# Key norms of the delta rule from ScalarE's row sums over token-major transposes, in place of half of TensorE's products with ones

## What is computed

```python
def l2_normalize(x):
    return x * lax.rsqrt(jnp.sum(x * x, axis=-1, keepdims=True) + NORM_EPS)
...
qkv_a = jax.nn.silu(causal_depthwise_conv(qkv_a, gdn_conv_w))
q_a, k_a, v_a = [a.reshape(b_, s_, GDN_HEADS, GDN_HEAD_DIM).astype(f32) for a in jnp.split(qkv_a, 3, axis=-1)]
q_a = l2_normalize(q_a) * (GDN_HEAD_DIM ** -0.5)
k_a = l2_normalize(k_a)
...
kb = k * beta[..., None]
a_low = jnp.where(strict, jnp.einsum('bhnid,bhnjd->bhnij', kb, k) * decay, 0.0)
ia = a_low + jnp.eye(c, dtype=q.dtype)
u = lax.linalg.triangular_solve(ia, v * beta[..., None], left_side=True, lower=True, unit_diagonal=True)
```

## Time and profile before

| What | Value |
|---|---|
| median of 3 runs | 890.04 us |
| the profiled execution | 890.07 us, its span 888.3 us |
| PE busy | 874.8 us (98%), 5624 instructions |
| DVE busy | 586.1 us (66%) |
| ACT busy | 440.2 us (50%) |
| POOL busy | 51.3 us (6%) |
| chain that ended last | PE 87%, DVE 8%, ACT 2%, issue 1%, DMA 1% |
| granted clock of PE, mean | 0.998 |

### The profile page before, as it was taken

How to read it: one execution, slowest core, us unless ns; L and a number is a source line. 1 busy time by engine, 2 the same in 40 slices (tenths; PEclk the granted TensorE clock), 3 DMA queues, 4 the chain that set the end, 5 groups by cost and what they waited for, 6 DMA issues and landing times.

```text
span 888.3 us, 13795 instructions
## 1 busy us (share of the span) xinstructions
PE 874.8 (98%) x5624; PEld 759.6 (86%) x5624; DVE 586.1 (66%) x898; ACT 440.2 (50%) x644; POOL 51.3 (6%) x78
## 2 busy tenths in 40 slices
PE   8999999999999999999999999999999999999997
PEld 6888999898999888888889999877788888888885
DVE  5785664565656755555686997956477667777544
ACT  6644444753345544544485652466254555555442
POOL 1000000000020110000020015200000100000000
PEclk9999999999999999999999999999999999999999
DMA  9757644456454554556757683412555556665441
GB/s 294 239 190 227 223 144 142 143 166 183 127 184 153 184 179 153 175 183 198 263 145 248 159 174 95 144 49 49 143 190 181 180 184 190 189 190 190 166 166 48
DMA packets 127813, 151.67 MB, mean 171 GB/s; under 512 B 16983, under 2 KB 93142, under 8 KB 127750
## 3 DMA queue, kind: packets, MB, share of 16 engines
q1 hardware_dynamic: 127466, 150.44, 53.8%
q10 hardware_dynamic: 220, 0.28, 0.1%
q0 software_dynamic: 64, 0.07, 0.0%
HBM read 148.67 MB, written 3.68 MB: 172 GB/s over the span
## 4 chain that ended last, share of the span: by engine, by line
PE 87%; DVE 8%; ACT 2%; issue 1%; DMA 1%; POOL 0%; POOLq 0%; SPq 0%; ACTq 0%; DVEq 0%
PE bank L519 18%; PE bank L521 17%; PE bank L520 17%; PE bank L1357 9%; PE bank L546 5%; PE bank L1360 5%; PE bank L548 2%; DVE w_lo L2141 2%; DVE arena L2553 1%; PE bank L1017 1%; PE bank L751 1%; PE bank L731 1%; PE bank L850 1%; DMA arena<-in_x 1%; PE bank L711 0%
## 5 line engine op out<-in xcount | busy, mean ns | idle before, releaser
L2141 DVE TENSOR_TENSOR w_lo<-ring,w_hi 128x2048 fp32r<-128x2048 f32 (+1 forms) x134 | 297.5, 2230 | 120.4 <-ACT w_hi L1566 120.0
L1566 ACT ACTIVATE w_hi<-ring 128x2048 fp32r<-128x2048 f32 (+1 forms) x134 | 249.1, 1861 | 93.0 <-PE bank L521 71.5
L519 PE MATMUL bank<-h_both,w_hi 128*128 128x256 f32 x488 | 140.3, 287 | 0.4 <-DVE w_lo L2141 0.4
L520 PE MATMUL bank<-h_both,w_hi 128*128 128x256 f32 x488 | 138.0, 283 | 0.0
L521 PE MATMUL bank<-h_both,w_lo 128*128 128x256 f32 x488 | 138.0, 283 | 0.0
L1357 PE MATMUL bank<-h_both,w_hi 128*128 128x512 f32 x352 | 96.5, 395 | 0.8 <-DVE arena L2867 0.8
L519 PEld LDWEIGHTS bank<-h_both,w_hi 128*128 128x128 f32 x488 | 93.5, 192 | 2.4 <-issue 1.4
L520 PEld LDWEIGHTS bank<-h_both,w_hi 128*128 128x128 f32 x488 | 93.6, 192 | 0.1
L521 PEld LDWEIGHTS bank<-h_both,w_lo 128*128 128x128 f32 x488 | 93.5, 192 | 0.0
L519 PE MATMUL bank<-w_hi,h_both 128*128 128x512 f32 (+1 forms) x192 | 73.7, 384 | 0.0
L521 PE MATMUL bank<-w_hi,h_both 128*128 128x512 f32 (+1 forms) x192 | 71.5, 372 | 0.0
(11 more groups left out here) (387 smaller groups left out, 1525.9 us busy)
## 6 DMA issues: line engine op xcount, KB each, us to landing
ring<-in_w_in SPq DMA_DIRECT2D x59, 1024.0 KB, 5.1
ring<-in_w_gate_up SPq DMA_DIRECT2D x44, 512.0 KB, 4.7
ring<-in_w_down SPq DMA_DIRECT2D x10, 1024.0 KB, 5.0
ring<-in_w_mem_kv SPq DMA_DIRECT2D x8, 1024.0 KB, 10.0
ring<-in_w_gla_out SPq DMA_DIRECT2D x4, 1024.0 KB, 5.0
ring<-in_w_x_out SPq DMA_DIRECT2D x4, 1024.0 KB, 5.2
ring<-in_w_dsa_out SPq DMA_DIRECT2D x4, 1024.0 KB, 5.2
ring<-in_w_o SPq DMA_DIRECT2D x4, 1024.0 KB, 4.9
```

Source lines behind the costliest of these rows:

```text
L519: mm(o, ah, bh, start=start, stop=False, skip_group_check=True)
L520: mm(o, ah, bl, start=False, stop=False, skip_group_check=True)
L1566: act(w_hi[:, k % NHI, at:m], ring[:, order.index(name) % NSLOT, at:m], ACT.Copy)\
L2141: tt_(w_lo[:, i, at:m], ring[:, i, at:m], w_hi[:, k % NHI, at:m].bitcast(F), ALU.subtract)\
```

## The change

The keys' transposes `kk0`, `kk1` move from behind `nq1` to right behind the `kg` products. ACT reads them there, squares each head's 128 columns and lets the instruction's accumulator give the row sum, straight into the key columns of `norm_cols` (eight instructions, in place of the two channel-major squares of the keys). PE's product with ones is kept for the queries alone (8 matmuls in place of 16). DVE adds epsilon to the query sums from the bank and to the key sums in place, in two instructions instead of one, the second behind a wait for ACT's eight squares.

```diff
             pe.wait_ge(signal("silu_done"), 4)
             head_products("kg", 4)
+            head_transposes("kk", 4)
             project_channels("nq0", h_parts)
-            pe.wait_ge(signal("squares"), 4)
+            pe.wait_ge(signal("squares"), 2)
             bank = open_bank("ss")
             for t in range(TT):
-                for i in range(8):
+                for i in range(4):
...
             project_channels("nq1", h_parts)
-            head_transposes("kk", 4)
             pe.wait_ge(*read("nq0"))
...
             conv_tanh(5)
-            square_of(2)
-            square_of(3)
             copy("kwvc", pair(ns, 1))
+            for t in range(TT):
+                sc.wait_ge(*full(f"kk{t}"))
+                for h in range(4):
+                    i = 8 * t + 4 + h
+                    act(sq[:, 4 + h, 128 * t:128 * t + 128], bank_of(f"kk{t}")[:, 128 * h:128 * h + 128], ACT.Square,
+                        accum_out=norm_cols[:, i:i + 1]).then_inc(signal("k_squares"), 1)
             sc.wait_ge(signal("d_min"), 1)
...
             bank_ready("ss")
-            tsc(norm_cols, bank_of("ss")[:, 0:16], 4 * EPS, None, ALU.add).then_inc(reader("ss"), 1)
+            q_sums = bank_of("ss")[:, 0:16].rearrange("p (t i) -> p t i", t=TT)[:, :, 0:4]
+            tsc(a_cols[:, :, 0:4], q_sums, 4 * EPS, None, ALU.add)
+            ve.wait_ge(signal("k_squares"), 8)
+            tsc(a_cols[:, :, 4:8], a_cols[:, :, 4:8], 4 * EPS, None, ALU.add).then_inc(reader("ss"), 1)
```

## The result

The changed kernel takes **897.06 us** (median of 6 runs, 896.37 to 897.28), the kernel before 890.03 us (6 runs, 889.73 to 890.46) beside it: ratio 1.0077 with a 95% interval of 1.0067 to 1.0087. It is slower by about 7 us; forecast were 896.6 us in a range of 894.4 to 899.5. The profiled execution took 896.83 us, its span is 894.9 us.

What follows compares the result with a forecast made beforehand. PE was taken to bound the kernel, busy 874.8 of 888.3 us, nearly balanced with DVE's chain. A wait leaving 4.7 us plus 1.8 us clock loss, 6.5 us on 890.07, gave 896.6 us, range 894.4 to 899.5.

Steps and rivals of the forecast that it cites:

- PE ready for `nq1`: On PE after the rope products: nq1 could start at 537.80, 0.96 us sooner than before, if its bank were free.
- Start of `nq1`: PE stands from 537.8 to 545.2, 7.4 us, until DVE's second read of kk0 gives back the bank.
- The squares: Eight key squares with accumulator on ACT, 0.38 us each, 3.04 us in all, done at 530.54.
- The sums of half the size gain the chain only 0.7 us: Norms' chain: POOL starts at 536.1 against 536.83, since ACT's squares delay the exponentials and with them DVE.
- The clock: At nq1 behind PE's wait: matmuls start at half rate, costing 1.8 us, bounded by nothing and 5.85 us.
- `hid` and the solve swallow 0.64 and 0.23 us: Earlier waits at hid and the first solve products absorb 0.64 and 0.23 us of the delay, leaving 4.7 us.
- the clock staying up: Rival at nq1: no clock loss, or what follows absorbs as much; 894.8 us, chance 0.15.
- the clock down throughout `nq1`: Rival: all of nq1 runs at half rate, costing 5.85 us; 900.6 us, chance 0.10.
- `kk0` is read in time: Rival: DVE gives back kk0 by 537.8, so nq1 need not wait; not slower, 889.3 us, chance 0.05.
- the squares take 0.50 us each: Rival on ACT: another 0.9 us on ACT, DVE and the wait; 897.5 us, or 899.3 with twice the clock's loss.

Runs made afterwards that it cites:

- e3: Changed kernel with seven unread identity products put into nq0's bank ahead of nq1, where PE otherwise stands: 894.56 us, ratio 1.0048.
- e7: The changed kernel unaltered, profiled once more for a second trace: 896.27 us (one run).
- e1: Changed kernel with transposes made twice: set `ka` for ACT's squares, `kk` for DVE again behind nq1: 889.28 us, ratio 0.9988 against the kernel before.
- e5: Changed kernel with transposes kk between nq0 and ss, DVE reading kk0 and kk1 right behind the column scales: 894.18 us, ratio 1.0045.
- e9: e5 with z0 and z1 low passes later, nA scaled ahead of the kk reads, POOL's first two level masks before its third rope product: 888.11 us.
- e8: e5 with DVE's low passes of z0 and z1 later and its kk0, kk1 reads behind the rope additions again: 889.24 us, ratio 0.9992.

## Why the prediction was right

It was right in its mechanism and its sum. The steps, each relative to `kg`:

- **PE ready for `nq1`: 537.80 forecast.** By the pitch of 2.29 us behind `qg` it was 536.26 - 0.74 + 2.29 = 537.81. The 1.84 us that `ss` loses and the 0.87 that `kk` adds ahead were nearly right (1.79 and 0.85).
- **Start of `nq1`: 545.2 forecast, 545.12 measured.** The wait of 7.4 us is 7.31 from start to start; the profile's 6.96 counts from the modelled end of the rope products.
- **The squares: 0.38 us each forecast, 0.25 measured.** ACT finished 0.9 us sooner than thought (530.40 - 0.74 = 529.66 against 530.54). It changed next to nothing, because of the next point.
- **"The sums of half the size gain the chain only 0.7 us ..., because ACT's squares now hold up the exponentials": the size was nearly right, the reason wrong.** POOL starts 0.88 us earlier than before (536.69 - 0.74 against 536.83). But DVE was through with its low pass, had the squares, and waited 0.64 us for PE's `ss`. Half of the gain is lost because the transposes (0.87 us) now stand ahead of `ss`, and not because of ACT. The forecast had both at nearly the same time, 535.62 and 535.7, and took the wrong one for the later. That two causes lay within 0.1 us of each other is why the wrong one gave the right size: luck.
- **The clock: 1.8 us forecast; 1.30 and 1.95 in the two traces, 2.6 by e3's ratio.** That the loss lies between nothing and all of `nq1` held. That 1.8 came so near is in part luck: it was read from one start, and the same working on the start of the trace after, whose six records at L654 start from 1.0 to 5.5 us, would have given about 2.3. The first trace has 0.5 us less of it, so its stretch grew by 5.9 us at the solve (565.14 - 0.74 - 558.46), not 6.5; that its span is 6.6 us longer is due to the late start. In e7 the stretch grew by 6.6 us (its first solve products start at 564.65, and `kg` is 0.40 early).
- **`hid` and the solve swallow 0.64 and 0.23 us: held in sum.** `r2` is 6.79 us later than before, `hid` 6.24 and the solve 5.94, so 0.55 and 0.30 us were swallowed, 0.85 for 0.87. No wait is left at either.

Of the rivals, the clock staying up is excluded by the granted clock, the clock down throughout `nq1` by the return at 549.16 and 549.34. "`kk0` is read in time" fell in this kernel, and its price of 889.3 was fair: e1, which has no such wait but makes the transposes twice, took 889.28. That the squares take 0.50 us each is excluded by the 0.25 measured.

What stays open: the medians differ by 7.03 us, the two traces explain 5.9 and 6.6. A run's mean granted clock does not settle it. It is 0.996 in the first trace and 0.994 in e7, although the lower clock behind the wait lasts as long in one as in the other; the two means differ because the clock falls again behind PE's last matmul, between 893 and 894 us in the first trace and between 890 and 891 in e7. The other five runs of the changed kernel (0.992 to 0.994) have no trace, so whether they lost more at `nq1` or elsewhere is not shown.

## What to carry to other kernels

Where results take turns in a fixed number of banks, producing one earlier does not only move its own cost: it takes a bank away until its last reader is done, so look up who opens that bank next and when the reader comes. If an early consumer needs the data long before the late one does, make it twice: 0.87 us of transposes bought back 7.8 us here (e1 against the change, from two sessions). Price a new wait on TensorE with the clock behind it, and before DVE work is reordered, look at what POOL does in the new place.

## What was not expected of the hardware

That DVE and POOL hold each other up was not in the forecast, and it made e5 fail: a 1.02 us pair of additions took 2.88 us, a low pass 3.36 for 2.29, and a POOL product 3.35 for 1.27. In these runs it showed where DVE read two tiles of SBUF: four reads with one input in PSUM kept a pitch of 0.60 us beside POOL's masks (e9), and the additions kept their 1.02 us where POOL stood (e8).

It could have been seen in the trace of the kernel before. There the first column scale, 128x8, took 1.25 us from 539.80, and the second 0.66, both beside POOL's first two rope products; the last, of the same operation and size as the second, took 0.16 us just after POOL had ended at 541.73:

```profile
539.75 1.98 POOL L2086 TENSOR_TENSOR arena<-arena 128x512 f32<-128x512 f32 x2
```

```profile
541.09 0.66 DVE L2603 SCALAR_TENSOR_TENSOR arena<-arena 128x8 f32<-128x8 f32 x1
...
541.87 0.16 DVE L2605 SCALAR_TENSOR_TENSOR arena<-arena 128x8 f32<-128x8 f32 x1
```

These scales lie in the very chain that `nq1` waits for in the changed kernel (1.23 us for the first, at 539.65). About 1.6 us of it, as an estimate from these rows, is DVE waiting for POOL; no run tried POOL's rope products elsewhere.

The kernel's start varies as well: a transfer that came late moved the whole span of the first trace of the changed kernel by 0.7 us (ACT's high pass behind it started at 15.54, in e7 at 14.87), which has to be taken off before terms are compared. The first six matmuls do not tell it: they took 4.54 us in the trace before, 5.47 in the first one after and 5.49 in e7, where `kg` was 0.40 us early.
